# Delta rule of one layer: the products and updates of each inversion level made only in the 32 of 64 columns that the level changes

## The reference, cut to what matters

```
def step(S, inp):
    r_t, w_t, k_t, v_t, kk_t, b_t = inp
    sa = jnp.einsum('bhvk,bhk->bhv', S, -kk_t)
    S = (S * w_t[:, :, None, :] + sa[..., None] * b_t[:, :, None, :]
         + v_t[..., None] * k_t[:, :, None, :])
    y = jnp.einsum('bhvk,bhk->bhv', S, r_t)
    return S, y
_, ys = lax.scan(step, S0, xs)
```

## Time and profile before

| what | value |
|---|---|
| median of 3 runs | 3045.92 us (3045.36 to 3047.9) |
| the profiled execution, its own time | 3045.94 us |
| its span in the profile | 3043.9 us |
| granted TensorE clock, mean over the span | 0.991 |
| PE busy / DVE busy / ACT busy | 2970.3 / 1820.8 / 1380.9 us |
| the inversion of tile 0 and of tile 1 | about 2738 to 2770 us and 2798 to 2828 us |

### The profile page before, as it was taken

One profiled execution on the slowest core, in us unless ns is written; L12 is line 12 of the kernel. 1 busy time (PEld: TensorE's weight loads), 2 busy tenths in 40 slices (PEclk: granted clock), 3 DMA queues, 4 the chain that ended last, 5 costly groups with the idle time before them and its releaser, 6 DMA issues.

```text
span 3043.9 us, 45964 instructions
## 1 busy us (share of the span) xinstructions
PE 2970.3 (98%) x17935; PEld 2468.6 (81%) x17935; DVE 1820.8 (60%) x2046; ACT 1380.9 (45%) x1900; POOL 337.8 (11%) x367
## 2 busy tenths in 40 slices
PE   9999999999999997999999999999999999998899
PEld 7888788788888886888888888888788887878787
DVE  5555657955766666555555555556544666666765
ACT  5555544343443447444434444444544445650244
POOL 2000010950000766200000000000000000000000
PEclk9999999999999997999999999999999999999999
DMA  6555475675667886566666565665666668660264
GB/s 229 173 171 171 152 210 198 223 232 182 191 204 224 241 261 192 163 190 212 186 194 188 190 188 187 193 187 182 183 180 193 183 197 247 186 202 10 99 221 166
DMA packets 300806, 576.82 MB, mean 190 GB/s; under 512 B 21417, under 2 KB 40105, under 8 KB 298945
## 3 DMA queue, kind: packets, MB, share of 16 engines
q1 hardware_dynamic: 284400, 521.27, 55.5%
q0 software_dynamic: 10992, 43.07, 4.9%
q10 hardware_dynamic: 5218, 9.68, 0.9%
HBM read 546.18 MB, written 21.50 MB: 186 GB/s over the span
## 4 chain that ended last, share of the span: by engine, by line
PE 91%; DVE 5%; ACT 2%; issue 1%; DMA 1%; POOL 0%; ACTq 0%; DVEq 0%; POOLq 0%; SPq 0%
PE acc L960 26%; PE acc L967 26%; PE acc L961 26%; PE tp L975 2%; DVE wL L2415 2%; PE acc L1681 1%; PE acc L1674 1%; PE acc L1675 1%; PE tp L1584 1%; PE acc L1582 1%; DMA raw<-in_mlp_w_dram 1%; PE wk L1260 0%; PE acc L1275 0%; ACT wH L1739 0%; PE acc L1276 0%
## 5 line engine op out<-in xcount | busy, mean ns | idle before, releaser
L2415 DVE TENSOR_TENSOR wL<-raw,wH 128x1024 fp32r<-128x1024 f32 (+1 forms) x968 | 1225.5, 1275 | 1089.0 <-ACT wH L1739 1086.9
L1739 ACT CAST wH<-raw 128x1024 fp32r<-128x1024 f32 (+1 forms) x968 | 1009.2, 1046 | 1382.1 <-PE acc L967 1172.5
L960 PE MATMUL acc<-wH,xH 128*128 128x512 f32 (+1 forms) x2208 | 867.4, 393 | 4.3 <-ACT wH L1739 3.3
L961 PE MATMUL acc<-wH,xL 128*128 128x512 f32 (+1 forms) x2208 | 856.3, 388 | 0.0
L967 PE MATMUL acc<-wL,xH 128*128 128x512 f32 (+1 forms) x2208 | 588.4, 388 | 1.6 <-DVE wL L2415 1.6
L960 PE MATMUL acc<-wH,hH 128*128 128x512 f32 x1472 | 577.9, 393 | 1.9 <-DVE hL L2469 1.9
L961 PE MATMUL acc<-wH,hL 128*128 128x512 f32 x1472 | 574.6, 390 | 0.0
L960 PEld LDWEIGHTS acc<-wH,xH 128*128 128x128 f32 x2208 | 415.4, 188 | 93.7 <-issue 7.3
L967 PEld LDWEIGHTS acc<-wL,xH 128*128 128x128 f32 x2208 | 413.2, 188 | 87.7 <-DVE wL L2415 2.4
L961 PEld LDWEIGHTS acc<-wH,xL 128*128 128x128 f32 x2208 | 415.7, 188 | 82.4 <-issue 0.5
L967 PE MATMUL acc<-wL,hH 128*128 128x512 f32 x1472 | 396.1, 391 | 5.3 <-DVE wL L2415 5.2
(11 more groups left out here) (512 smaller groups left out, 2214.7 us busy)
## 6 DMA issues: line engine op xcount, KB each, us to landing
raw<-in_mlp_w_dram SPq DMA_DIRECT2D x512, 512.0 KB, 3.8
raw<-in_w_in_dram SPq DMA_DIRECT2D x192, 512.0 KB, 3.9
raw<-in_a_w_in_dram SPq DMA_DIRECT2D x96, 512.0 KB, 3.8
raw<-in_b_w_glu_dram SPq DMA_DIRECT2D x64, 512.0 KB, 3.7
raw<-in_a_w_out_dram SPq DMA_DIRECT2D x32, 512.0 KB, 3.7
raw<-in_w_out_dram SPq DMA_DIRECT2D x32, 512.0 KB, 4.3
raw<-in_w_proj_fox_dram SPq DMA_DIRECT2D x16, 512.0 KB, 5.3
raw<-in_w_proj_rwkv_dram SPq DMA_DIRECT2D x16, 512.0 KB, 4.7
```

Source lines behind the costliest of these rows:

```text
L960: nc.tensor.matmul(bank, aH[:, k, rows], wH[:, j % SPLIT, u, 0:n], start=k == 0, stop=False)
L961: nc.tensor.matmul(bank, aL[:, k, rows], wH[:, j % SPLIT, u, 0:n], start=False, stop=False)
L1739: nc.scalar.copy(wH[:, j % SPLIT, :, 0:n], raw[:, j % RAW, :, 0:n]).then_inc(high_done, 1)
L2415: nc.vector.tensor_tensor(wL[:, j % SPLIT, :, 0:n], raw[:, j % RAW, :, 0:n], wH[:, j % SPLIT, :, 0:n].bitcast(F32), ALU.subtract).then_inc ...
```

## The change

In the inversion, an operand or result of 64 columns becomes one of 32 where the level leaves the other 32 as they are. `blocks_of(t, lv, e)` takes the first (e = 0) or second (e = 1) block of each pair, 64 / 2w pieces of w columns; `compact` puts the result into the first 32 columns of the head's place in the bank. Q of level 1 and its mask stay whole, so that all of QQ is written once. From level 2 on QQ's other columns keep old numbers; as weights in the transposed product these give rows of the result which the update must leave out. So the update of XT becomes one scalar_tensor_tensor, XT + factor * product, with a factor by partition: -1 in the rows that the level changes and 0 in the others. The factors (tile upper, [128, 5]) are made once from the masks, by two DVE instructions put behind the wait for them at the end of the second MLP.

```diff
--- before.py
+++ after.py
@@ -390,6 +390,7 @@
         shift = sb("shift", [P, P])
         corner = sb("corner", [P, P])
         level = sb("level", [P, LEVELS + 2, P])
+        upper = sb("upper", [P, LEVELS])
         fstat = sb("fstat", [P, 8])
         DG = da_groups()
         dpe_names, dact_names, ddve_names = da_steps()
@@ -459,6 +460,7 @@
         relu_done = sem("relu_done")
         const_a = sem("const_a")
         const_b = sem("const_b")
+        upper_made = sem("upper_made")
         mask_step = sem("mask_step")
         lam_in = sem("lam_in")
         lam_step = sem("lam_step")
@@ -1532,6 +1534,9 @@
             nat = lambda h: 2 * (h % 8) + h // 8
             head = lambda h: slice(nat(h) * R_HD, (nat(h) + 1) * R_HD)
 
+            blocks_of = lambda t, lv, e: t.rearrange("p (n e w) -> p n e w", e=2, w=1 << lv)[:, :, e]
+            compact = lambda o, lv: o[:, 0:TC // 2].rearrange("p (n w) -> p n w", w=1 << lv)
+
             for m in range(MT):
                 for j in range(4):
 
@@ -1570,8 +1575,10 @@
                         wait(name_dve=("X", m, lv - 1, k) if lv > 1 else ("xi", m, k))
                         for h in range(8 * k, 8 * k + 8):
                             for c in range(2):
-                                last = nc.tensor.matmul(B[k][half[c], (h % 8) * TC:(h % 8 + 1) * TC], A4[k][half[c], h % 8, 0],
-                                                        XA[half[c], h], start=True, stop=True)
+                                o, x = B[k][half[c], (h % 8) * TC:(h % 8 + 1) * TC], XA[half[c], h]
+                                if lv > 1:
+                                    o, x = compact(o, lv), blocks_of(x, lv, 0)
+                                last = nc.tensor.matmul(o, A4[k][half[c], h % 8, 0], x, start=True, stop=True)
                         RPE.mark(r_pe, last, "Q", m, lv, k)
                     for k in range(2):
                         wait(name_dve=("Q", m, lv, k))
@@ -1579,9 +1586,11 @@
                             cols = slice((h % 8) * TC, (h % 8 + 1) * TC)
                             if lv < LEVELS:
                                 for c in range(2):
-                                    nc.tensor.matmul(B[2 + k][half[c], cols], XT[half[c], h], QQ[half[c], h], start=True, stop=True)
+                                    nc.tensor.matmul(compact(B[2 + k][half[c], cols], lv), XT[half[c], h], blocks_of(QQ[half[c], h], lv, 0),
+                                                     start=True, stop=True)
                             for c in range(2):
-                                last = nc.tensor.matmul(B[4 + k][half[c], cols], QQ[half[c], h], XT[half[c], h], start=True, stop=True)
+                                last = nc.tensor.matmul(compact(B[4 + k][half[c], cols], lv), QQ[half[c], h], blocks_of(XT[half[c], h], lv, 1),
+                                                        start=True, stop=True)
                         RPE.mark(r_pe, last, "XQ", m, lv, k)
                 wait(("AV", m, 1), ("XT", m, LEVELS, 1))
                 for name, b0 in (("U", 0), ("W", 2)):
@@ -2986,6 +2995,9 @@
 
             mlp(tail=both_gains)
             dve.wait_ge(mask_step, MASK_STEPS)
+            nc.vector.tensor_reduce(upper[:], level[:, 2:2 + LEVELS, 0:TC], AX, ALU.max).then_inc(upper_made, 1)
+            dve.wait_ge(upper_made, 1)
+            nc.vector.tensor_scalar(upper[:], upper[:], -1.0, None, ALU.add).then_inc(upper_made, 1)
 
             lead_ends()
             for q in range(QT):
@@ -3112,6 +3124,8 @@
             wide = lambda t: t.unsqueeze(2).broadcast_to([P, R_HEADS, R_HD])
             over = lambda t: t.unsqueeze(1).broadcast_to([P, 8, TC])
             eight = lambda b: b.rearrange("p (a t) -> p a t", a=8)
+            blocks_of = lambda t, lv, e: t.rearrange("p h (n e w) -> p h n e w", e=2, w=1 << lv)[:, :, :, e]
+            compact = lambda b, lv: eight(b)[:, :, 0:TC // 2].rearrange("p h (n w) -> p h n w", w=1 << lv)
             TT = nc.vector.tensor_tensor
 
             def step(ins, *name):
@@ -3294,13 +3308,22 @@
                     for k in range(2):
                         h8 = slice(8 * k, 8 * k + 8)
                         dve.wait_ge(r_pe, RPE["Q", m, lv, k])
-                        step(TT(QQ[:, h8], eight(B[k]), over(level[:, lv + 1, 0:TC]), ALU.mult), "Q", m, lv, k)
+                        if lv == 1:
+                            step(TT(QQ[:, h8], eight(B[k]), over(level[:, 2, 0:TC]), ALU.mult), "Q", m, lv, k)
+                        else:
+                            keep = blocks_of(level[:, lv + 1, 0:TC].unsqueeze(1), lv, 0).broadcast_to([P, 8, TC >> (lv + 1), 1 << lv])
+                            step(TT(blocks_of(QQ[:, h8], lv, 0), compact(B[k], lv), keep, ALU.mult), "Q", m, lv, k)
                     for k in range(2):
                         h8 = slice(8 * k, 8 * k + 8)
                         dve.wait_ge(r_pe, RPE["XQ", m, lv, k])
                         if lv < LEVELS:
-                            step(TT(XA[:, h8], XA[:, h8], eight(B[2 + k]), ALU.subtract), "X", m, lv, k)
-                        step(TT(XT[:, h8], XT[:, h8], eight(B[4 + k]), ALU.subtract), "XT", m, lv, k)
+                            x = blocks_of(XA[:, h8], lv, 0)
+                            step(TT(x, x, compact(B[2 + k], lv), ALU.subtract), "X", m, lv, k)
+                        if lv == 1:
+                            dve.wait_ge(upper_made, 2)
+                        x = blocks_of(XT[:, h8], lv, 1)
+                        step(nc.vector.scalar_tensor_tensor(x, compact(B[4 + k], lv), upper[:, lv - 1:lv], x, ALU.mult, ALU.add),
+                             "XT", m, lv, k)
                 if m:
                     end_mean(0)
                     end_centre(0)
```

## The result

| | before | after |
|---|---|---|
| median of 4 runs each, side by side | 3046.91 us (3045.36 to 3048.21) | 3079.98 us (3077.46 to 3083.69) |
| span of the profiled execution | 3043.9 us | 3078.4 us |
| granted clock, mean over the span | 0.991 | 0.975 |

The ratio is 1.011, with a 95% interval of 1.0098 to 1.0123: the change makes the kernel 33 us slower. 3038.7 with a range of 3031 to 3044 was forecast, so the sign is wrong too.

The account below looks back on a forecast made before the run. The ring of PE and DVE in the two inversions was taken as the bound; 3.7 us saved a tile, 7.4 for both, less 0.2 for the low clock, gave 3045.9 - 7.2 = 3038.7 us, range 3031 to 3044.

Parts of the forecast that it names:

- TensorE's clock falls: Rival: PE streams half the columns, so the granted clock drops in one tile's inversion, 22 us more, 3061 us; chance 0.11.
- Against it: PE issues as densely as before, and its rest in a level gets shorter: Argument in the inversion levels that the granted clock would not drop; no size of its own.
- the 0.2 us in the sum "for the low clock": Deduction for tile 0's level 1, part of which runs at the low clock, where narrower products gain nothing; 0.2 us.
- PE's 4.1 us: Share of the 7.2 us saving in both inversions from PE's products losing 5 ns per quarter of the array.
- So 64 fp32 weight columns want 53 ns in their quarter [...] Of the 58.3 ns only 5 can go: Inversion products: weight load limits each array quarter, so pace between loads falls from 29.1 to 26.6 ns.
- PE is halved: Rival: in the inversions the stream sets PE's pace and loads hide behind it; saves 21 us, 3025 us; chance 0.08.
- The 106 ns for 128 weight columns: Time per matmul with two moving columns, taken as nearly pure weight load at 0.81 ns a column.
- DVE's 3.1 us: Share of the 7.2 us saving from DVE's chain of updates and mask leaving the path in both inversions.
- the 1.6 a tile of the sum: DVE's saving per inversion at PE's old pace: 0.35 us in four levels plus 0.22 in the tail.
- Only DVE's part comes (3042.5): Rival: in the inversions PE keeps 29.1 ns, or pieces slow DVE; about 3.1 to 3.5 us saved; chance 0.17.
- Nothing comes: Rival: something behind the inversions has its own time, so nothing is saved, 3046 us; chance 0.04.
- The factors: Two DVE instructions before the split at the second MLP's end: 0.5 and 0.2 us, costing nothing.

Follow-up runs that it names:

- DVE alone: The changed kernel with all PE products at 64 moving columns again, DVE's masks and updates kept at 256 elements; 3042.0 us, ratio 0.9988.

## Why the prediction was wrong

**The clock.** The rival *TensorE's clock falls* is what happened, and it had 0.11. Its price was right: 22 us for an inversion at 1.2 GHz, levels of 10.2 us, measured 10.24. It was counted for one tile; for both it gives 3038.7 + 44 = 3083, and 3080.0 was measured. That closeness is part luck, as the 22 us are counted from a high-clock pace that the kernel doesn't reach: in tile 1 the low clock cost 45.06 - 24.99 = 20.1. The step that failed is its "Against it: PE issues as densely as before, and its rest in a level gets shorter", together with the 0.2 us in the sum "for the low clock". The earlier trace rows and the 0.95 of the earlier trace rows showed that the clock falls at the entry of level 1 already before the change; I priced that stretch and never asked what brings the clock back out of it. The runs answer in three steps: the pause causes the fall (filled, it doesn't come), 64- and 48-column products end it in 3.4 us, and products of 32 columns, the engine busy without a gap, don't end it in the 43 and 45 us that they run. The low stretch that begins at the entry, by the kind of the products (in the first row only XQ of level 1 falls into it, so 32 / 64 is there no test of Q at 32):

| Q / XQ | low for, us |
|---|---|
| 64 / 64, 48 / 48, 32 / 64 | 3.4 |
| 64 / 32 | 6.8 and 10.2 |
| 32 / 32 in levels 1 and 2, then 64 | 20.5 |
| 32 / 32 | 47.8, the last 5.0 or 2.7 of it in 64-column products behind |
| 32 / 32 from level 2 on, 64 in level 1 | 3.4 |
| 32 / 32, pause filled | 0 |

Whether the clock falls at an entry differs from one execution and tile to the next: in the profiled executions of the twelve kernels that keep the pause it fell in 18 of 24 inversions, in the two with the pause filled in 0 of 4. The four times of the changed kernel, 3077 to 3084, say that it fell in both tiles each time. Why a pause of the same length sometimes does not cost the clock is open; so is what TensorE's activity is measured by, of which the runs only show that a busy share of 1.00 is not it.

**The likeliest forecast, PE's 4.1 us.** It was worth 0. The step that failed is "So 64 fp32 weight columns want 53 ns in their quarter [...] Of the 58.3 ns only 5 can go". That the load sets the pace is right, and *PE is halved* was rightly put low. But the 5 ns isn't a rest of the stream that a shorter stream gives back: 64x32 has it too, and 32x32 has it on top of 27 (nearly 32 in a quarter). The 106 ns for 128 weight columns misled me: I put all of it down to the columns, and so left no fixed part. The earlier trace rows spoke against it already: at half the clock a rest of the stream would have doubled with the load, to 2 x 58.3 = 117 ns in a quarter, and the row gives 107. The Trainium skill (TensorE: Matmul & The Clock Gate, Wait — 56ns, not 53.3ns?) gives about 2.5 ns fixed for every matmul at the high clock, and none at the low one. Counting a load like a matmul, an estimate from this figure is 2 x 2.5 = 5 ns. The trace agrees at the low clock, 106.6 ns in a quarter, which is 2 x 53.3 with nothing on top; no run here splits the 5 ns between load and matmul.

**DVE's 3.1 us.** Right in mechanism, and in size as the traces show it. 256-element rows at 0.42 and 0.48 us also in pieces of two columns, levels of 5.60 with the clock up, 26.57 to 24.99 in tile 1, which is the 1.6 a tile of the sum. The medians can't confirm the size: they lie 5.5 us below the kernel before for DVE alone and 5.0 for the change with the pause filled, and their intervals reach from 0.9 to 6.4 and from 2.7 to 8.5. So with the clock aside *Only DVE's part comes (3042.5)* was the true case: DVE alone gave 3042.0 and the change with the pause filled 3041.7, where the closeness is luck in part, since the kernel before stood higher beside them (3047.5 and 3046.7) than the 3045.9 of the sum. Its reason wasn't the right one either: a short stream does cost less (16 ns for 28 with 32 weight columns), and here the load of 64 hides it. *Nothing comes* falls with these. The stretch behind the inversions has no time of its own, since the changed kernel hands on all but 2.6 of its 37.1 us to the end.

**The factors.** 0.5 and 0.2 us forecast, 0.48 and 0.17 measured, hidden as said.

## What to carry to other kernels

Before a product is made narrower, look what its load costs: with 64 fp32 weight columns, 32 moving ones take the same 29 ns as 64, and only both sides narrow go faster (16 ns). If the profile shows even a short stretch at the low clock, find what ends it, for a change that makes TensorE's work thinner there can turn 3.4 us into 48. A few products nobody reads, put into the pause ahead, can be worth trying: they took 38 us off the changed kernel, and 0.7, which the noise hides, off one whose 64-column products end the low stretch anyway. And judge TensorE by the granted clock and the count of instructions in a stretch, never by its busy share, which was at its highest where the work went slowest.

## What the runs showed of the hardware that was not expected

- The clock has a memory: the same 32-column products ran through four and five levels at 1.00 when it was up, and through five levels at 0.50 when it was down. The Trainium skill (TensorE: Matmul & The Clock Gate, What's actually happening) says that a throttled TensorE is released by being kept busy. The trace agrees for 64 columns (back in 3.4 us), and for 32 it doesn't if busy is what the profile calls so: 30.00 of 30.00 us at 0.50.
- A pause of 1.96 us between dense products can be enough for a fall: it came in 18 of 24 inversions. The same page of the Trainium skill (HAM oscillation — how this bites in real kernels) warns of idle gaps, but of longer ones than this.
- The duration of a matmul in the profile hardly shows how much it streams, and busy time doesn't either. With 64 weight columns it is 219 ns for 32 moving columns and 218 for 64 at the high clock, and 291 and 312 at the low one; with 32 weight columns it is 193 and 217 at the high clock.
- DVE takes pieces of two fp32 columns in steps of four nearly at the price of one piece: the updates of XA, level 1 with its pieces of two among them, all take 420 to 423 ns for 256 elements, against 414 in the earlier trace rows.
